# The end of a decoder block: sums put into banks by identity products, and ten more constant products in its head

## What is computed

```python
mod = (jax.nn.silu(c) @ w_ada[l] + b_ada[l])[:, None, :]
sh1, sc1, gt1, sh2, sc2, gt2 = jnp.split(mod, 6, axis=-1)
h = rmsnorm(x, g_pre_mix[l]) * (1.0 + sc1) + sh1
...
y = hier_moe(h, w_group[l], b_group[l], w_router[l], b_router[l], w_gate[l], w_up[l], w_down[l])
x = x + gt2 * rmsnorm(y, g_post_ffn[l])
```

## Time and profile before

| | |
|---|---|
| median of 3 runs | 1563.5 us (1561.81 to 1564.2) |
| profiled execution | 1562.75 us |
| its span in the trace | 1560.4 us |
| TensorE / VectorE / ScalarE / GpSimd busy | 1511.8 / 681.7 / 231.8 / 41.2 us |
| moved by DMA | 589.96 MB, mean 378 GB/s |
| chain that ended last | PE 71%, DMA 22%, SPq 3%, DVE 3% |

### The profile page before, as it was taken

One profiled execution on the slowest core, in us unless ns is written; L12 is line 12 of the kernel. 1 busy time (PEld: TensorE's weight loads), 2 busy tenths in 40 slices (PEclk: granted clock), 3 DMA queues, 4 the chain that ended last, 5 costly groups with the idle time before them and its releaser, 6 DMA issues.

```text
span 1560.4 us, 19229 instructions
## 1 busy us (share of the span) xinstructions
PE 1511.8 (97%) x7984; PEld 811.9 (52%) x7984; DVE 681.7 (44%) x1228; ACT 231.8 (15%) x443; POOL 41.2 (3%) x57
## 2 busy tenths in 40 slices
PE   4999999999999999999999999999999999999996
PEld 2888888855654446344344344344444434434432
DVE  3565757676877635232232232232232332322325
ACT  2100311111232303011011011011011010010003
POOL 2000000000001200000000000000000000000003
PEclk9999999999999999999999999999999999999999
DMA  9999567699878996899999999999999999999994
GB/s 360 398 385 374 208 259 300 251 361 365 307 301 293 365 411 248 357 428 428 428 428 428 429 429 428 428 428 430 404 429 429 427 428 430 430 428 427 429 429 179
DMA packets 102323, 589.96 MB, mean 378 GB/s; under 512 B 5745, under 2 KB 16465, under 8 KB 76929
## 3 DMA queue, kind: packets, MB, share of 16 engines
q1 hardware_dynamic: 99904, 580.93, 91.7%
q0 software_dynamic: 1696, 5.66, 1.0%
q10 hardware_dynamic: 672, 2.66, 0.5%
HBM read 587.07 MB, written 2.16 MB: 378 GB/s over the span
## 4 chain that ended last, share of the span: by engine, by line
PE 71%; DMA 22%; SPq 3%; DVE 3%; issue 0%; ACTq 0%; ACT 0%; DVEq 0%
PE bank L1163 21%; DMA ring<-in_w_up 20%; PE bank L1196 8%; PE bank L923 7%; PE bank L673 5%; PE bank L639 5%; PE bank L1077 4%; PE bank L864 4%; PE bank L1057 3%; SPq L380 2%; DMA ring<-in_w_ada 2%; PE bank L707 2%; PE bank L686 1%; PE bank L689 1%; DMA ring<-in_w_in 1%; PE bank L1088 1%
## 5 line engine op out<-in xcount | busy, mean ns | idle before, releaser
L1163 PE MATMUL bank<-ring,RN 128*64 128x512 f32 x1488 | 330.6, 593 | 7.9 <-DMA ring<-in_w_up 7.9
L1163 PEld LDWEIGHTS bank<-ring,RN 128*64 128x64 f32 x1488 | 106.7, 137 | 220.7 <-issue 200.2
L1196 PE MATMUL bank<-ring,RN 128*64 128x512 f32 x992 | 219.7, 595 | 0.5 <-issue 0.5
L2212 DVE TENSOR_TENSOR RN<-bank,RN 64x512 f32<-64x512 f32 x31 | 21.5, 693 | 374.0 <-ACT RN L1517 374.0
L1196 PEld LDWEIGHTS bank<-ring,RN 128*64 128x64 f32 x992 | 68.9, 137 | 137.4 <-issue 135.6
L2219 DVE COPY RG<-bank 64x512 f32<-64x512 f32 x64 | 44.1, 689 | 196.1 <-PE bank L1196 188.4
L1057 PEld LDWEIGHTS bank<-RN,RX 128*128 128x128 f32 x976 | 111.5, 192 | 13.0 <-issue 13.0
L1057 PE MATMUL bank<-RN,RX 128*128 128x128 f32 x976 | 115.7, 277 | 0.0
L923 PE MATMUL bank<-ring,RT 128*128 128x512 f32 x256 | 113.0, 596 | 0.8 <-DVE RT L1999 0.8
L1163 PE MATMUL bank<-RT,RN 128*64 128x512 f32 x256 | 112.3, 592 | 0.0
L1077 PE MATMUL bank<-RG,RN 128*128 128x512 f32 x240 | 109.5, 599 | 0.0
(11 more groups left out here) (395 smaller groups left out, 1474.8 us busy)
## 6 DMA issues: line engine op xcount, KB each, us to landing
ring<-in_w_down SPq DMA_DIRECT2D x64, 2048.0 KB, 15.4
ring<-in_w_up SPq DMA_DIRECT2D x48, 2048.0 KB, 20.2
ring<-in_w_gate SPq DMA_DIRECT2D x47, 2048.0 KB, 16.0
ring<-in_w_ada SPq DMA_DIRECT2D x32, 2048.0 KB, 10.4
ring<-in_w_in SPq DMA_DIRECT2D x18, 2048.0 KB, 9.2
RT<-in_w_gate SPq DMA_DIRECT2D x17, 2048.0 KB, 15.5
RH<-in_w_up SPq DMA_DIRECT2D x16, 2048.0 KB, 20.0
ring<-in_w_ada SPq DMA_DIRECT2D x18, 1024.0 KB, 18.5
```

The costliest lines, as they stand in the source:

```text
L1163: last = mm(bank[0][64 * s:64 * s + 64, :], tokT[:, k, q * CAP:(q + 1) * CAP], w[:, k % 8, :], start=k == 0, stop=k == KT - 1, skip_group_ ...
L1196: last = mm(bank[2 + n % 2][64 * (n // 2):64 * (n // 2) + 64, :], hidT[:, k * CAP:(k + 1) * CAP], wdn[:, n * BLK:(n + 1) * BLK], start=k = ...
```

## The change

In the head, 28 constant products instead of 18 stand ahead of the second chunk's column sums.

At the end, the old sum of tile 1 (`ysum[:, 1]`) is put into four banks by products with the identity (`carried`): one piece in place of the first clock-keeping group of `last_expert`, one in place of the second, two behind the last expert. Tile 1's scatter products then add to these banks (`start=tt == 0`), and VectorE adds nothing for tile 1. Tile 0's pieces go into banks 7, 1, 2, 3, tile 1's into 5, 6, 0, 4, so that no scatter product waits for a bank.

ScalarE squares tile 1's pieces straight from their banks, and VectorE multiplies them from there with the gain, each behind its square. GpSimd multiplies tile 0's four pieces only. Tile 0's root is taken behind the fifth square, and VectorE scales the identity by its reciprocal (`root_diag`). Behind the scatter products TensorE waits for all four multiplied pieces of tile 0 and then makes x * rstd + y in the banks of tile 0: per piece one product of the identity with `y` and one of the scaled identity with `x_t`. ScalarE copies the four banks out, each after its pair of products. VectorE makes the sums of tile 1 only. SP's order of stores becomes: tile 0 left, tile 0 right, tile 1 left, tile 1's two last pieces.

```diff
@@ -100,6 +100,7 @@
 C_TWO, C_COLS = 865, 905
 
 LAST_COLS = (0, 2, 1, 3)
+SUM_BANKS = [(7, 1, 2, 3), (5, 6, 0, 4)]
 V_C, V_BADA, V_GPRE1 = 0, 16, 112
 V_LB0, V_LB1, V_PEK, V_PEV, V_ROWS = 0, 8, 16, 48, 80
 
@@ -537,8 +538,8 @@
                     sp.sem_inc(sig("dense_here").sem, 1)
             with sp.Else():
                 sp.nop()
-            for name, n, tt, c0, c1 in (("out_ready", 1, 0, 0, 1024), ("out_ready", 2, 1, 0, 1024), ("pool_out", 1, 0, 1024, D),
-                                        ("out_ready", 3, 1, 1024, 1536), ("out_ready", 4, 1, 1536, D)):
+            for name, n, tt, c0, c1 in (("first_out", 2, 0, 0, 1024), ("first_out", 4, 0, 1024, D), ("out_ready", 1, 1, 0, 1024),
+                                        ("out_ready", 2, 1, 1024, 1536), ("out_ready", 3, 1, 1536, D)):
                 sp.wait_ge(sig(name).sem, n)
                 sp.dma_start(out[tt * P:(tt + 1) * P, c0:c1], x_t[:, tt, c0:c1]).then_inc(sig("stored").sem, 16)
             sp.wait_ge(sig("stored").sem, 80)
@@ -588,7 +589,7 @@
                 k0, n = CHUNKS[c]
                 if c > 0:
                     wait(pe, "mod_copied", c)
-                    constant_products((18, 8, 0, 0)[c - 1])
+                    constant_products((28, 8, 0, 0)[c - 1])
                 pe.wait_ge(sig("part_ready").sem, c + 1)
                 if c == 0:
                     wait(pe, "shift_row")
@@ -1077,6 +1078,12 @@
                     mm(bank[4 + i % 4][:, :], ohwT[:, tt * P:(tt + 1) * P], rows[:, c * BLK:(c + 1) * BLK],
                        start=True, stop=True).then_inc(sig("scattered").sem, 1)
 
+            def carried(pieces):
+
+                for i in pieces:
+                    c0 = LAST_COLS[i] * BLK
+                    mm(bank[SUM_BANKS[1][i]][:, :], ident, ysum[:, 1, c0:c0 + BLK], start=True, stop=False, skip_group_check=True)
+
             def last_expert(p):
 
                 e = 2 * p + 1
@@ -1092,12 +1099,12 @@
                 for tt in range(TT):
                     last = tr(bank[7][:, tt * P:(tt + 1) * P], ohw[:, tt, :], ident)
                 last.then_inc(sig("ohwT").sem, 1)
-                keep_clock(2, 5)
+                carried((0,))
                 pe.wait_ge(sig("hidden").sem, e + 1)
                 for f in range(4):
                     last = tr(bank[1][:, f * P:(f + 1) * P], hid[:, f:4 * P:4], ident)
                 last.then_inc(sig("hiddenT").sem, 1)
-                keep_clock(3, 5)
+                carried((1,))
                 pe.wait_ge(sig("rows_copied").sem, e * 2 + 2)
                 pe.wait_ge(sig("hiddenT_copied").sem, e + 1)
                 for b, ks in ((0, (0, 1)), (1, (0, 1)), (0, (2, 3)), (1, (2, 3))):
@@ -1120,10 +1127,8 @@
                         pe.wait_ge(sig("last_rows").sem, i + 1)
                     if i == 2:
                         pe.wait_ge(sig("rows_copied").sem, n * 4 + 1)
-                    if i >= 4:
-                        pe.wait_ge(sig("scatter_added").sem, (n - 1) * 8 + (i - 3))
-                    mm(bank[4 + i % 4][:, :], ohwT[:, tt * P:(tt + 1) * P], rows[:, c * BLK:(c + 1) * BLK],
-                       start=True, stop=True).then_inc(sig("scattered").sem, 1)
+                    mm(bank[SUM_BANKS[tt][i % 4]][:, :], ohwT[:, tt * P:(tt + 1) * P], rows[:, c * BLK:(c + 1) * BLK],
+                       start=tt == 0, stop=True, skip_group_check=True).then_inc(sig("scattered").sem, 1)
 
             def pair(p, gather_next, scatter_last=True):
                 for q in range(2):
@@ -1202,6 +1207,7 @@
             with pe.Fori(1, NE // 2 - 1) as p:
                 pair(p, True)
             pair(NE // 2 - 1, False)
+            carried((2, 3))
 
 
             wait(pe, "flag_ready")
@@ -1245,9 +1251,18 @@
                         last.then_inc(sig("dense_down").sem, 1)
                         pe.wait_ge(sig("dense_added").sem, c + 1)
                     pe.sem_inc(sig("dense_used").sem, 1)
+                carried(range(4))
             with pe.Else():
                 pe.nop()
             last_scatter(NE // 2)
+            pe.wait_ge(sig("scatter_added").sem, 8 * (NE // 2 - 1) + 4)
+            pe.wait_ge(sig("gained").sem, 4)
+            for i in (0, 2, 1, 3):
+                c0 = LAST_COLS[i] * BLK
+                mm(bank[SUM_BANKS[0][i]][:, :], ident, y[:, 0, c0:c0 + BLK], start=True, stop=False)
+                if i == 0:
+                    wait(pe, "root_diag")
+                mm(bank[SUM_BANKS[0][i]][:, :], sil[:, 0:P], x_t[:, 0, c0:c0 + BLK], start=False, stop=True).then_inc(sig("first_sums").sem, 1)
 
 
         @block.scalar
@@ -1552,17 +1567,22 @@
             act.nop()
             do(fn(st[:, 12:13], ones[:, 0:1], ACT.Sqrt))
             for i in range(8):
-                act.wait_ge(sig("scatter_added").sem, 8 * (NE // 2 - 1) + i + 1)
                 c0 = LAST_COLS[i % 4] * BLK
-                do(fn(ring[:, 4, :, :].rearrange("p a b -> p (a b)")[:, i * BLK:(i + 1) * BLK], ysum[:, i // 4, c0:c0 + BLK], ACT.Square,
+                if i < 4:
+                    act.wait_ge(sig("scatter_added").sem, 8 * (NE // 2 - 1) + i + 1)
+                    of = ysum[:, 0, c0:c0 + BLK]
+                else:
+                    act.wait_ge(sig("scattered").sem, 8 * (NE // 2 - 1) + i + 1)
+                    of = bank[SUM_BANKS[1][i - 4]][:, :]
+                do(fn(ring[:, 4, :, :].rearrange("p a b -> p (a b)")[:, i * BLK:(i + 1) * BLK], of, ACT.Square,
                       accum_out=st[:, 20 + i:21 + i]), sig("ysum_squares"))
-                if i == 7:
-                    act.wait_ge(sig("gained").sem, 4)
-                    act.wait_ge(sig("first_rstd").sem, 1)
-                    do(fn(x_t[:, 0, 1024:D], x_t[:, 0, 1024:D], ACT.Copy, scale=st[:, 8:9]), sig("first_scaled"))
                 if i in (4, 7):
                     wait(act, f"ysum_var{i // 6}")
                     do(fn(st[:, 8 + i // 6:9 + i // 6], st[:, 8 + i // 6:9 + i // 6], ACT.Sqrt), sig(f"ysum_sd{i // 6}"))
+            for c, i in enumerate((0, 2, 1, 3)):
+                c0 = LAST_COLS[i] * BLK
+                act.wait_ge(sig("first_sums").sem, c + 1)
+                do(fn(x_t[:, 0, c0:c0 + BLK], bank[SUM_BANKS[0][i]][:, :], ACT.Copy), sig("first_out"))
 
 
         @block.gpsimd
@@ -1640,15 +1660,11 @@
             pool.dma_start(RG[:, 1, :], late_rows[3 * KT:4 * KT, :].rearrange("(o k) p -> o (k p)", o=1).to_broadcast([P, D]))\
                 .then_inc(sig("gain2_in").sem, 16)
             wait(pool, "gain2_in", 16)
-            for i in range(6):
+            for i in range(4):
                 pool.wait_ge(sig("scatter_added").sem, 8 * (NE // 2 - 1) + i + 1)
-                c0 = LAST_COLS[i % 4] * BLK
-                nc.gpsimd.tensor_tensor(x_t[:, i // 4, c0:c0 + BLK], ysum[:, i // 4, c0:c0 + BLK], RG[:, 1, c0:c0 + BLK], ALU.mult)\
+                c0 = LAST_COLS[i] * BLK
+                nc.gpsimd.tensor_tensor(x_t[:, 0, c0:c0 + BLK], ysum[:, 0, c0:c0 + BLK], RG[:, 1, c0:c0 + BLK], ALU.mult)\
                     .then_inc(sig("gained").sem, 1)
-            pool.wait_ge(sig("first_scaled").sem, 1)
-            for c0 in (1024, 1536):
-                ins = nc.gpsimd.tensor_tensor(x_t[:, 0, c0:c0 + BLK], x_t[:, 0, c0:c0 + BLK], y[:, 0, c0:c0 + BLK], ALU.add)
-            ins.then_inc(sig("pool_out").sem, 1)
 
 
         @block.vector
@@ -2274,23 +2290,20 @@
             for i in range(8):
                 dve.wait_ge(sig("scattered").sem, 8 * (NE // 2 - 1) + i + 1)
                 c0 = LAST_COLS[i % 4] * BLK
-                w = ysum[:, i // 4, c0:c0 + BLK]
-                tt_op(w, w, bank[4 + i % 4][:, :], ALU.add).then_inc(sig("scatter_added").sem, 1)
-                if i == 4:
-                    last_var(0)
-                if i == 6:
+                if i in (4, 7):
+                    last_var(i // 5)
+                if i == 5:
                     last_rstd(0)
-            dve.wait_ge(sig("gained").sem, 3)
-            last_sum(0, 0, 1024)
-            do(tt_op(x_t[:, 1, BLK:2 * BLK], ysum[:, 1, BLK:2 * BLK], RG[:, 1, BLK:2 * BLK], ALU.mult))
-            last_var(1)
+                    step(ts(sil[:, 0:P], ident, st[:, 8:9], None, ALU.mult), "root_diag")
+                if i < 4:
+                    w = ysum[:, 0, c0:c0 + BLK]
+                    tt_op(w, w, bank[SUM_BANKS[0][i]][:, :], ALU.add).then_inc(sig("scatter_added").sem, 1)
+                else:
+                    dve.wait_ge(sig("ysum_squares").sem, i + 1)
+                    do(tt_op(x_t[:, 1, c0:c0 + BLK], bank[SUM_BANKS[1][i - 4]][:, :], RG[:, 1, c0:c0 + BLK], ALU.mult))
             last_rstd(1)
-            dve.wait_ge(sig("gained").sem, 5)
             last_sum(1, 0, 1024)
-            do(tt_op(x_t[:, 1, 3 * BLK:D], ysum[:, 1, 3 * BLK:D], RG[:, 1, 3 * BLK:D], ALU.mult))
-            dve.wait_ge(sig("gained").sem, 6)
             last_sum(1, 1024, 1536)
-            settle()
             last_sum(1, 1536, D)
 
 
```

## The result

The changed kernel's median is 1565.44 us (20 runs, 1563.35 to 1569.08) against 1563.4 us for the kernel before (20 runs). The ratio is 1.0015, 95% interval 1.0008 to 1.0021: 2.3 us slower (1.3 to 3.3), within the 0.2% called "same". The profiled execution took 1564.48 us with a span of 1562.4; what the time has beyond the span is 2.1 us, against 2.35 before, so the execution is 1.7 us longer and the span 2.0.

A forecast was written before the change was run, and what follows sets the result against it. TensorE or the transfers work all the time, so savings count only on TensorE's sequence, its waits or behind its last product. Head −0.93 and end +3.3 give +2.4 on the median 1563.5: 1565.9 us, range 1563.0 to 1568.0.

The forecast's parts named there:

- part 1: Head: ten more constant products fill TensorE's gap and keep the clock, next block 0.93 us earlier (bounds +0.77, −1.1).
- part 2: Last expert: two identity products replace the clock-keeping groups; transposes start 0.20 us later, +0.20 in sum (bounds 0 and 0.3).
- part 3: Behind the down products: two identity products that nothing hides delay the scatter by 1.72 us (1.34 to 1.72).
- tail: Time from the start of the scatter products to the end of the span; forecast 20.8 us, 19.4 before.
- asking at 103.9 leaves 0.2 us: Second column sums: VectorE's sum, ready at 103.67, would still come 0.2 us before TensorE asks for it.
- I let it through whole: Behind the second column sums: the head's 0.93 us gain was taken to run undiminished through the next 1400 us.
- the first rival: Head gain lost at the column sums at 103.9 or weight streams: 1566.8; with the falling clock 1567.6, together chance 0.33.
- the rival's other place: The streams of weights behind the column sums, where the 0.93 us might be lost waiting for transfers; shared chance 0.33.
- Parts 4 to 6: End: tile 0's last products and copies done at 1557.7, tile 1's sums at 1556.1, stores ending at 1563.7.
- 1557.7 + 0.8 + 3.9 + 1.3: Stores: tile 0's last piece ready, delay to first bytes, transfer of four stores, rest to the span's end: 1563.7.
- Faster, by products of one record: Identity products take one pass, not two records; tile 1's last sum then sets the end: 1560.4, chance 0.07.
- The clock falling in spite of the products: Head: the clock drops despite the added products, costing +0.77, with the end +4.1: 1567.6; within the slower chance 0.33.

## Why the prediction was right, and where it was not

The whole: 1565.9 was forecast and 1565.44 measured, +2.4 against +2.0 by the medians and +2.3 by the ratio, inside "same". The two parts measured alone (−0.8 and +3.0 against −0.93 and +3.3) bear the mechanism out. Point by point, in the traces:

| step | forecast | measured |
|---|---|---|
| part 1, head, next block | −0.93 | −0.81 |
| part 1, carried through | −0.93 | −0.37 at 109, −0.47 at 618 |
| from 618 to the last expert | 0 | −0.78 |
| part 2 | +0.20 | +0.09 |
| part 3 | +1.72 (from 1.34) | +1.59 |
| tail | 20.8 us, +1.4 | 20.99 us, +1.57 |
| span | +2.4 | +2.0 |

The five measured steps (−0.47, −0.78, +0.09, +1.59, +1.57) add up to the +2.0. Without the −0.78, for which the forecast had nothing, they give +2.8; so in this one trace two misses, a head gain half lost and a stretch that happened to be short, partly cancel, and that its span lies near the forecast is partly luck. The 20 runs rest on no single trace.

*Part 1.* The clock came back as the chunk at 104.83 had promised. The step that was too large is "asking at 103.9 leaves 0.2 us" and "I let it through whole": VectorE's sum of the second chunk came at 104.3 and not at 103.7, and TensorE waited. The margin of 0.2 us was smaller than the movement of that sum, which ended TensorE's wait at 103.97, 104.11, 104.25 and 104.36 in the four profiled executions whose rows show one. VectorE's last addition of that chunk ended between 103.55 and 104.45 in the ten other executions and at 104.25 in the changed kernel's, in two of those with 28 products about when it ended in the kernel before (103.55 and 103.72 against 103.67), so the later column sums alone do not move it. In the changed kernel it runs with hardly a break from 93.72, where a transfer of w_ada rows ends its wait, and the chain goes through this transfer; with 28 products alone and with the stores reordered it stays on TensorE. What moves the transfer is open. The second column sums were the place named in the first rival, and about half of the gain ended there. From there to 618 the rest went through whole, also as forecast; the streams behind, the rival's other place, took nothing in that stretch.

*From 618 to the last expert* nothing was forecast, and 0.78 us were found. Whether they are the change's is open. The time between the transfers of up weights that start at 1070 and at 1473 (1069.71 and 1472.54 in the chain shown) is 402.83 us in the changed kernel and 403.63 before; it was 402.93 in the kernel with 28 products alone, 402.76 with the stores reordered, 402.36 without the y products, 404.10 in the changed kernel with 18 products and 404.68 in the kernel before with 25, by their chains. In the other four it was 402.71 (two carried pieces), 402.62 (tile 0 stored in four pieces), 402.69 (21 products) and 402.87 (two carried pieces, 25 products). So kernels whose code is the same in that stretch differ by 2.3 us, and the two with 25 products by 1.8; but all six with 28 products are under 403 and both with 18 over it, which one execution of each can't tell from chance. TensorE's waits for up weights in it come to 2.4 us in the changed kernel and 2.8 before, 1.9 in the shortest and 3.6 in the longest. It is the stretch in which the order of the loads changes (`IN_ORDER`) and TensorE bounds for a while. What decides it in one execution is open. This, and the 1.6 us between 618 and 1070 in the kernel with 28 products alone, is why a single span can't tell the parts apart, and the tail can.

*Part 2* was hidden better than thought: the transposes came 0.20 later, as forecast, but ran 0.12 us faster behind the larger product (0.63 for 0.75). From the one-hot's transposes to the down products it is 2.75 us (1529.83 to 1532.58) against 2.66 before (1531.08 to 1533.74).

*Part 3.* Two products that nothing hides, bounded at 1.34 to 1.72. The five kernels that make them have 8.83 or 8.84 us from down to scatter products, the six without 7.06 to 7.49. Against that whole range the price is 1.3 to 1.8 us, and the bounds can't be told apart. TensorE's own work in it is 6.86 + 1.72 = 8.58, which leaves 0.25 us beyond it, where the kernels without the products have 0.20 to 0.63; that part of the branch's overhead runs beside the products isn't shown. The experiment with two carried pieces removed it.

*Parts 4 to 6.* Restart forecast at scatter start + 7.0, measured 7.09; last copy 14.8, 14.83. That these eight products set it is shown by the kernel without four of them (11.49, tail 17.56). Tile 1 was done at 12.04, over a microsecond earlier than the 13.2 of the forecast (1556.1 less 1542.9), since the scaled identity stood at 7.03 and not at 7.4, its sums took 2.61 us and not 3.06, and what lies between (2.40 us) was forecast at 2.7; it does not matter, as these stores wait. That they wait behind tile 0 right, and that this costs, is shown by the change of the order alone: tail 18.0. "1557.7 + 0.8 + 3.9 + 1.3" measured from the last copy's end: 6.16 us against 6.0. The first multiplication out of a bank (L2303, 1547.31) took 0.69 us beside GpSimd, as forecast: no price.

VectorE's scaling of the identity is recorded as 0.33 us from 1548.11, so it began 0.25 us before GpSimd's last multiplication ended (1543.39 + 4.97 = 1548.36) and ended 0.08 behind that end. The seven kernels that scale the identity show more: it begins 0.24 to 0.30 us before GpSimd's end and lasts 0.328 to 0.386 us, the longer the earlier it begins, and its end lies 0.083 to 0.088 us behind GpSimd's in all seven. Its end is tied to GpSimd's, though no run has the scaling without GpSimd beside it. The Trainium skill's "SBUF — State Buffer", section "Who interferes with whom", gives a full block for two-port forms, which scaling by a scalar can take, and the traces agree as far as they go. It costs little: the spread of the seven is 0.06 us, and elsewhere, with GpSimd idle, a scaling of 128x64 (L2176 of the kernel before) takes 0.31 us and one of 128x256 (L1729) 0.41.

*The rivals.* Faster, by products of one record: the carried products are two records each (L1085 x2 for one, x4 for two), 0.857 us; out. The clock falling in spite of the products: out with 28 and 25, and not in general, as the kernel with 21 shows at its second chunk.

## What to carry to other kernels

A queue that issues stores in a written order needs that order to follow readiness in the new kernel, not in the old one: three finished stores behind an unfinished one cost 3.0 us, as much as the whole change of the end lost. Work put on the busiest engine is free only in the places where it already waits: two identity products in place of clock-keeping ones cost 0.09 us together, two behind the last expert 1.6 (1.3 to 1.8). And a gain on one engine reaches only as far as the next sum of another engine: look up that one's readiness and how much it moves from run to run, before counting the gain whole.

## What was not expected of the hardware

Whether the granted clock falls around the column sums is not told by the idle time ahead of them. It fell after gaps of 2.3 and 1.75 us at the first column sums, and at the second after 0.51 us (21 products, clock 0.64, 14 records in 4.79 us); it stood after 0.76 us at the first, and at the second after 0.43 and 0.86 us, in kernels that differ only in constant products and at the end. The level in the fall is 1.2 GHz, half the full clock (granted clock 0.50 in 76.0 to 78.5 in the kernel before and in 107.4 to 109.4 with 21 products), and it cost 1.7 us each time (4.96 for 3.27 us). Before it fell, the clock was 1.00 through the gap and through the column sums. What besides the gap decides it is open; no run was made for it, and one profiled execution of each of two kernels with 25 and of six with 28 products is too little to say that these numbers keep the clock always.
